# The end of a two-block transformer kernel weighted between panels and turned behind the last one, the even RMS norm multiplied in one operation, and four layer-norm shifts as one rounded product

## The reference, cut to what matters

```python
def layer_norm(x, g, b):
    mu = jnp.mean(x, -1, keepdims=True)
    var = jnp.mean(jnp.square(x - mu), -1, keepdims=True)
    return (x - mu) * lax.rsqrt(var + LN_EPS) * g + b
...
def rmsnorm(x, g):
    y = xf * lax.rsqrt(jnp.mean(xf * xf, axis=-1, keepdims=True) + EPS)
    return (y * g.astype(jnp.float32)).astype(x.dtype)
...
    for l in range(DEPTH):
        hl = rmsnorm(xl, norm_g[l]) * (1.0 + scale[:, None]) + shift[:, None]
        ...
        xl = xl + gate[:, None] * out_l.astype(xl.dtype)
    return rmsnorm(xl, final_g)
```

## Time and profile before

| | us |
|---|---|
| median of 3 runs | 2527.7 (2525.87 to 2528.76) |
| the profiled execution's own time | 2529.48 |
| its span | 2527.7 |
| PE busy | 2487.7 (98% of the span) |
| DVE, POOL, ACT busy | 1450.2, 1081.8, 955.5 |
| mean granted clock of PE | 0.997 |

### The profile page before, as it was taken

How to read it: one execution, slowest core, us unless ns; L and a number is a source line. 1 busy time by engine, 2 the same in 40 slices (tenths; PEclk the granted TensorE clock), 3 DMA queues, 4 the chain that set the end, 5 groups by cost and what they waited for, 6 DMA issues and landing times.

```text
span 2527.7 us, 34143 instructions
## 1 busy us (share of the span) xinstructions
PE 2487.7 (98%) x12624; PEld 2006.3 (79%) x12624; DVE 1450.2 (57%) x2058; ACT 955.5 (38%) x1500; POOL 1081.8 (43%) x718
## 2 busy tenths in 40 slices
PE   8999999999999999999999999999999999999999
PEld 7888887667788887788888877788888888787887
DVE  6545456575765645554555658674343364896553
ACT  5222224554522223432222568653222244463322
POOL 3978874313776735243343402264020056032401
PEclk9999999999999999999999999999999999999999
DMA  8345445311444446244443221145333326533332
GB/s 213 92 128 153 127 123 132 104 23 55 133 130 145 124 134 159 89 134 148 131 125 111 81 80 42 44 149 167 109 108 92 94 76 194 188 124 113 92 92 66
DMA packets 439258, 292.05 MB, mean 116 GB/s; under 512 B 34371, under 2 KB 420218, under 8 KB 435802
## 3 DMA queue, kind: packets, MB, share of 16 engines
q1 hardware_dynamic: 422042, 212.38, 29.9%
q0 software_dynamic: 17088, 77.93, 9.9%
HBM read 272.50 MB, written 20.92 MB: 116 GB/s over the span
## 4 chain that ended last, share of the span: by engine, by line
PE 87%; POOL 5%; DVE 3%; ACT 2%; DMA 1%; issue 1%; SPq 0%; ACTq 0%; POOLq 0%; DVEq 0%
PE ps L784 40%; PE ps L789 20%; PE ps L867 5%; PE ps L895 4%; PE ps L1096 2%; PE ps L1084 2%; POOL SW L3177 1%; POOL NS L3175 1%; PE ps L1532 1%; POOL NS L3174 1%; DMA raw<-in_ffn_w_down 1%; PE ps L1111 1%; PE ps L1385 1%; PE ps L1103 1%; POOL BK L3177 1%
## 5 line engine op out<-in xcount | busy, mean ns | idle before, releaser
L2330 DVE TENSOR_TENSOR wl<-raw,wh 128x1024 fp32r<-128x1024 f32 x376 | 623.6, 1659 | 830.2 <-ACT wh L1758 829.7
L1758 ACT ACTIVATE wh<-raw 128x1024 fp32r<-128x1024 f32 x385 | 408.2, 1060 | 1305.4 <-PE ps L789 1149.7
L784 PE MATMUL ps<-XH,wh 128*128 128x512 f32 x1832 | 718.5, 392 | 0.5 <-ACT wh L1758 0.5
L784 PE MATMUL ps<-XL,wh 128*128 128x512 f32 x1832 | 713.1, 389 | 0.0
L789 PE MATMUL ps<-XH,wl 128*128 128x512 f32 x1832 | 453.2, 389 | 0.0
L784 PEld LDWEIGHTS ps<-XH,wh 128*128 128x128 f32 x1832 | 343.9, 188 | 77.0 <-issue 4.9
L784 PEld LDWEIGHTS ps<-XL,wh 128*128 128x128 f32 x1832 | 343.9, 188 | 72.9 <-issue 2.2
L789 PEld LDWEIGHTS ps<-XH,wl 128*128 128x128 f32 x1832 | 343.8, 188 | 71.7 <-issue 0.4
L3296 POOL TENSOR_TENSOR NS<-AW,CS 128x2048 f32<-128x2048 f32 x32 | 117.7, 3679 | 272.7 <-PE ps L789 233.3
L784 PE MATMUL ps<-HH,wh 128*128 128x512 f32 x528 | 207.3, 393 | 2.2 <-ACT wh L1758 2.2
L784 PE MATMUL ps<-HL,wh 128*128 128x512 f32 x528 | 205.5, 389 | 0.0
(11 more groups left out here) (544 smaller groups left out, 3925.0 us busy)
## 6 DMA issues: line engine op xcount, KB each, us to landing
raw<-in_ffn_w_gu SPq DMA_DIRECT2D x176, 512.0 KB, 3.9
raw<-in_ffn_w_down SPq DMA_DIRECT2D x64, 512.0 KB, 3.9
AW<-in_ada_w POOLq DMA_DIRECT2D x24, 1024.0 KB, 6.5
raw<-in_ffn_w_down SPq DMA_DIRECT2D x32, 384.0 KB, 3.4
BS<-s_b POOLq DMA_DIRECT2D x12, 1024.0 KB, 5.3
raw<-in_odd_w_in SPq DMA_DIRECT2D x24, 512.0 KB, 3.8
raw<-in_even_w_in SPq DMA_DIRECT2D x22, 512.0 KB, 4.5
s_w<-SW POOLq DMA_DIRECT2D x12, 512.0 KB, 6.5
```

The lines of the kernel that those rows point to most:

```text
L784: pe.matmul(ps[:, p % 4, 0:n], wh[:, p % 2, k * P:(k + 1) * P], x[:, k, 0:n], start=k == 0 and x is hi, stop=False)
L1758: act.activation(wh[:, p % 2, :], raw[:, p % 4, :], ACT.Copy).then_inc(w_hi, 1)
L2330: dve.tensor_tensor(wl[:, p % 2, :], raw[:, p % 4, :], wh[:, p % 2, :].bitcast(F32), ALU.subtract).then_inc(w_lo, 1)
```

## The change

Three edits. None adds or removes a panel.

1. **Four shifts.** For ffn0 to ffn3 (not wo0 and wo1) ACT rounds block 0 of `XT` into `XH[:, 0, :]`, which no product reads by then, and PE multiplies it with a rounded column of 1/128 (`PART`, written once by ACT ahead of the first shift): a single-pass fp32r product for a float32 one. PE waits for a new semaphore, `first_hi`. So that the number of semaphores stays, `cmask_in` is merged into `mla_in_s`.
2. **Even RMS norm.** DVE makes `NT = XT * AG * factor` in one operation (no affine behind it). ACT makes `XH = round(NT + MOD)` and, for the even blocks, `NT = NT + MOD` in place for POOL. For the odd blocks DVE makes `XL = (NT + MOD) - XH` in one operation. POOL takes four blocks and DVE four, where it was six and two.
3. **The end.** Behind each panel's square ACT multiplies the block by `final_g` into `XG` (the tile `YO`); DVE does the last block. Behind the last panel PE transposes blocks 0 to 2 at once, then reduces the square of block 7, then transposes blocks 3 to 7; the reductions give one column per 128 tokens (tokens on partitions), so that square root and reciprocal are 128x4 and the spread is gone. The factor is applied behind the transposes, as tokens then lie on partitions: DVE for token blocks 0 and 2, ACT for 1 and 3, in three pieces each (3, 2 and 3 channel blocks). Four DMAs, one for each 128 tokens, 512 KB with rows of 4 KB. The `warm` products there are gone.

```diff
 # PE, shift(stage, j)
-                pe.matmul(ps[:, 4, :], EPS[:, 3:4].broadcast_to([P, P]), XT[:, 0, :], start=True, stop=True).then_inc(ln_mean, 1)
+                if stage in SHIFT_HI:
+                    pe.wait_ge(first_hi, SHIFT_HI.index(stage) + 1)
+                    pe.matmul(ps[:, 4, :], PART[:].broadcast_to([P, P]), XH[:, 0, :], start=True, stop=True).then_inc(ln_mean, 1)
+                else:
+                    pe.matmul(ps[:, 4, :], EPS[:, 3:4].broadcast_to([P, P]), XT[:, 0, :], start=True, stop=True).then_inc(ln_mean, 1)
 # ACT, behind(stage, p, j)
                 if j < KD - 1:
                     cast(BASE[stage] + p + 2)
+                if j == 0 and stage in SHIFT_HI:
+                    if stage == "ffn0":
+                        act.activation(PART[:], EPS[:, 3:4], ACT.Copy)
+                    act.wait_ge(*taken_at(stage, p))
+                    act.activation(XH[:, 0, :], XT[:, 0, :], ACT.Copy).then_inc(first_hi, 1)
 # ACT, rms: the even norm
-                    act.activation(XH[:, d, :], src[:, d, :], ACT.Identity, scale=AG[:, layer, d, 0:1],
-                                   bias=MOD[:, layer, d, 0:1]).then_inc(ln_hi, 1)
+                    if layer == 0:
+                        act.activation(XH[:, d, :], src[:, d, :], ACT.Identity, bias=MOD[:, layer, d, 0:1]).then_inc(ln_hi, 1)
+                        if d not in EVEN_BY_DVE:
+                            act.activation(src[:, d, :], src[:, d, :], ACT.Identity, bias=MOD[:, layer, d, 0:1]).then_inc(ln_aff, 2)
...
 # DVE, rms: the even norm, EVEN_BY_DVE = (1, 3, 5, 7)
+                for d in range(KD + 2 if layer == 0 else 0):
+                    if d < KD:
+                        dve.scalar_tensor_tensor(dst[:, d, :], XT[:, d, :], AG[:, 0, d, 0:1], ps[:, 4, :], ALU.mult, ALU.mult).then_inc(ln_n, 1)
+                    if d - 2 in EVEN_BY_DVE:
+                        dve.wait_ge(ln_hi, 8 * hi + d - 1)
+                        dve.scalar_tensor_tensor(XL[:, d - 2, :], dst[:, d - 2, :], MOD[:, 0, d - 2, 0:1], XH[:, d - 2, :].bitcast(F32), ALU.add, ALU.subtract).then_inc(x_dve, 1)
 # PE, the end: square_columns() is column_means(ACQ) in the place of rms_sum("final")
+            def column_means(src, first, last):
+                for t in range(TT):
+                    mm = pe.matmul(ps[:, 5, t:t + 1], src[:, t * P:(t + 1) * P], ONES[:, 0:1], start=first and t == 0, stop=last and t == TT - 1)
+                return mm
...
+            for d in range(3):
+                turned(d)
+            pe.wait_ge(sq_ready, LN_SQ["final"] + KD)
+            column_means(SQ[:, (LN_SQ["final"] + KD - 1) % 2, :], False, True).then_inc(sq_used, 1)
+            for d in range(3, KD):
+                turned(d)
 # ACT, the end (weighted(at) runs behind each square)
+                if d < KD - 1:
+                    act.activation(XG[:, d, :], XT[:, d, :], ACT.Identity, scale=COL[:, 96 + 64 + d:96 + 65 + d]).then_inc(ln_aff, 1)
+                else:
+                    turned_out(0)
+                    turned_out(2)
...
+            for t in (1, 3):
+                act.activation(XO[:, t, 0:3 * P], XO[:, t, 0:3 * P], ACT.Identity, scale=RSTD[:, t:t + 1])
+            for t in (1, 3):
+                act.wait_ge(out_ps, 5)
+                act.activation(XO[:, t, 3 * P:5 * P].rearrange("p (i c) -> p i c", c=P), turned_rows(3, 2, t), ACT.Identity, scale=RSTD[:, t:t + 1])
+            for t in (1, 3):
+                act.wait_ge(out_ps, KD)
+                act.activation(XO[:, t, 5 * P:].rearrange("p (i c) -> p i c", c=P), turned_rows(5, 3, t), ACT.Identity, scale=RSTD[:, t:t + 1]).then_inc(out_sb, 1)
 # DVE, the end: block 7's weight, the copy of block 1, a 128x4 reciprocal, then the same three pieces for t in (0, 2)
+            dve.tensor_scalar(XG[:, KD - 1, :], XT[:, KD - 1, :], COL[:, 96 + 64 + KD - 1:96 + 64 + KD], None, ALU.mult).then_inc(ln_n, 1)
+            dve.wait_ge(out_ps, 2)
+            dve.tensor_copy(XO[:, :, P:2 * P], ps[:, OUT_BANK[1], :].rearrange("p (t c) -> p t c", t=TT)).then_inc(ln_n, 1)
+            reciprocal(width=TT)
...
 # SP
-            for half in range(2):
-                sp.wait_ge(out_sb, 4 * half + 4)
-                sp.dma_start(rows_out[:, :, half * T:(half + 1) * T], XO[:, :, half * T:(half + 1) * T]).then_inc(out_done, 16)
-            sp.wait_ge(out_done, 32)
+            for t in range(TT):
+                sp.wait_ge(*((ln_n, LAST_N + 3 + t // 2) if t % 2 == 0 else (out_sb, 3 + t // 2)))
+                sp.dma_start(rows_out[:, t, :], XO[:, t, :]).then_inc(out_done, 16)
+            sp.wait_ge(out_done, 16 * TT)
```

More of the change, by code:

```diff
@@ L487, in program @@
         g_out = sem("g_out")
-        cmask_in = sem("cmask_in")
+        first_hi = sem("first_hi")
         qs_hi = sem("qs_hi")
@@ L546, in program @@
         ROOT_NO = {"ffn0": 1, "wo0": 4, "ffn1": 5, "ffn2": 6, "wo1": 7, "ffn3": 8, "even": 9, "odd": 10, "final": 11}
+        SHIFT_HI = ("ffn0", "ffn1", "ffn2", "ffn3")
         SHIFT_AT = {"ffn0": 1, "wo0": 2, "ffn1": 1, "ffn2": 1, "wo1": 3, "ffn3": 1}
@@ L564, in program @@
         XS = {"ffn0": 0, "mla": 8, "wo0": 14, "ffn1": 22, "kv": 28, "ffn2": 28, "nsa": 34, "wo1": 40, "ffn3": 48, "even": 54,
-              "glu": 60, "odd": 66}
-        XD = {"mla": 0, "ffn1": 2, "kv": 4, "ffn2": 4, "nsa": 6, "ffn3": 8, "even": 10, "odd": 12}
+              "glu": 58, "odd": 64}
+        XD = {"mla": 0, "ffn1": 2, "kv": 4, "ffn2": 4, "nsa": 6, "ffn3": 8, "even": 10, "odd": 14}
         BY_DVE = (3, 7)
+        EVEN_BY_DVE = (1, 3, 5, 7)
         LN_COL = {"ffn0": 0, "wo0": 8, "ffn1": 16, "ffn2": 24, "wo1": 32, "ffn3": 40}
@@ L599, in program, with out_at, turned_rows @@
         T_BANK = (1, 6)
+        XG = YO
+        LAST_N = 8 * LN_NO["final"]
+        OUT_BANK = (4, 6, 7)
+        def out_at(d, t):
+            if d < 3:
+                return OUT_BANK[d], t * P
+            first, i = ((0, 1), d - 3) if d < 5 else ((2, 6), d - 5)
+            return first[t % 2] + i // 2, i % 2 * 2 * P + t // 2 * P
+        def turned_rows(d, count, t):
+            bank, col = out_at(d, t)
+            return ps[:].rearrange("p b c -> p (b c)")[:, bank * T + col - t // 2 * P:][:, 0:count * 2 * P].rearrange("p (i h c) -> p i h c", h=2, c=P)[:, :, t // 2]
         block = ctx.enter_context(nc.Block())
@@ L929, in all_of @@
                 def all_of(k):
-                    if stage in XD and k in BY_DVE:
-                        return x_dve, XD[stage] + BY_DVE.index(k) + 1
-                    return x_split, XS[stage] + k + 1 - (sum(e < k for e in BY_DVE) if stage in XD else 0)
+                    by_dve = () if stage not in XD else EVEN_BY_DVE if stage == "even" else BY_DVE
+                    if k in by_dve:
+                        return x_dve, XD[stage] + by_dve.index(k) + 1
+                    return x_split, XS[stage] + k + 1 - sum(e < k for e in by_dve)
                 if stage == "ffn0":
@@ L1861, in rms @@
                 act.wait_ge(sq_used, PE_SQ[stage] + (1 if stage in ADDED else KD))
-                act.activation(ROOT, ps[:, 5, 0:P], ACT.Sqrt, bias=EPS[:, 2:3]).then_inc(sd_ready, 1)
+                width = P if layer is not None or wout is None else TT
+                act.activation(ROOT[:, 0:width], ps[:, 5, 0:width], ACT.Sqrt, bias=EPS[:, 2:3]).then_inc(sd_ready, 1)
                 beside("root")
@@ L2316, in _, with turned_out, weighted @@
                 take("odd", 16 + j, ZO[:, j % 2, :], ACT.Silu)
-            rms("final", lambda d: taken_at("owo", d), wout="owo")
-            for d in range(KD):
+            def turned_out(d):
                 act.wait_ge(out_ps, d + 1)
-                act.activation(XO[:, :, d * P:(d + 1) * P], ps[:, (6, 7, 0, 1)[d % 4], :].rearrange("p (t c) -> p t c", t=TT), ACT.Copy).then_inc(out_sb, 1)
+                act.activation(XO[:, :, d * P:(d + 1) * P], ps[:, OUT_BANK[d], :].rearrange("p (t c) -> p t c", t=TT), ACT.Copy).then_inc(out_sb, 1)
+            def weighted(at):
+                if at[0] != "square":
+                    return
+                d = at[1]
+                if d < KD - 1:
+                    act.activation(XG[:, d, :], XT[:, d, :], ACT.Identity, scale=COL[:, 96 + 64 + d:96 + 65 + d]).then_inc(ln_aff, 1)
+                else:
+                    turned_out(0)
+                    turned_out(2)
+            rms("final", lambda d: taken_at("owo", d), wout="owo", beside=weighted)
+            act.wait_ge(rstd_ready, ROOT_NO["final"])
+            act.wait_ge(out_sb, 2)
+            act.wait_ge(ln_n, LAST_N + 2)
+            for t in (1, 3):
[6 more added lines that the diff above has]
+                act.activation(XO[:, t, 5 * P:].rearrange("p (i c) -> p i c", c=P), turned_rows(5, 3, t), ACT.Identity, scale=RSTD[:, t:t + 1]).then_inc(out_sb, 1)
         @block.vector
@@ L3322, in _ @@
             norm("ffn2")
-            pool.wait_ge(cmask_in, 16)
+            pool.wait_ge(mla_in_s, 96)
             def rest_of_q(j, q):
```

57 lines of the change are left out of this document (35 added, 22 removed).

## The result

The changed kernel takes 2533.52 us (median of 9 runs, 2532.42 to 2537.28) against 2526.07 us for the kernel before on the same chip (9 runs, 2525.63 to 2528.76). The ratio is 1.003, 95% interval [1.0021, 1.0039]: slower, by 7.5 us in the medians. The forecast was 2521.7 and faster. The profiled executions took 2536.54 and, before, 2529.48: both some 3 us over their medians, and 7.1 apart.

A forecast was written before the change was run, and what follows sets the result against it. PE, busy 98% of the span, was taken as the bound. 1.4 + 2.8 + 2.7 = 6.9 us saved gave 2522.6 from the profiled execution or 2520.8 from the median; the middle, 2521.7, was forecast, 8-in-10 range 2517.8 to 2525.5.

The forecast's parts named there:

- the price of the new tile: Shift in ffn0: ACT writing PART takes 0.20 us, cutting that shift's net saving to 0.32; nothing counted for PART's place.
- Part 1: Four shifts: rounded product saves PE time less a new wait; 0.32 + 0 + 0.52 + 0.52 = 1.4 us.
- rivals: Clock stays up (0.2), even norm stays late (0.2), change doesn't do what it says (0.1), transfers don't overlap (0.05).
- PE's 2.25 in ffn1 not grown: ffn1: an earlier PE waits longer than 2.25 us for a late weight panel; no growth would show the forecast wrong.
- Even norm: Pair of panels behind the even norm: 15.47 us becomes 12.7, no waits, 3.4 us of low clock; gain 2.8.
- the old 4.5 of loss: Old even pair: 11.0 us of matmuls plus 1.1 of waits plus 3.4 lost to the low clock makes 15.5.
- a slack of 0.1 to 0.9: New even pair: DVE has each XL block ready 0.1 to 0.9 us before PE wants it, so no wait.
- The rival that the clock stays up: Even pair: PE has no idle time left, the clock doesn't fall; gain 8.6 us, time 2520.0; chance 0.2.
- End: Behind the last panel: first transfer issued at 2517.5 instead of 2520.31, span end at 2524.9; gain taken as 2.7 us.
- The rival of transfers that don't overlap: End: four 512 KB transfers of 3.9 us each run one after another; slower, 2530.3 us; chance 0.05.

The follow-up runs named there:

- e1: The changed kernel with all three edits, but PART a column of ST, so that no tile moves: 2519.27 us, ratio 0.997 against the kernel before.
- e2: The kernel before with only a dead tile of 32 bytes per partition where the change puts PART, no edits: 2542.16 us, ratio 1.0065.
- e5: The kernel before with the shifts edit alone, PART a column of ST, no tile moved: 2525.39 us, ratio 0.9993.
- e12: All three edits, no tile moved but YH and YL, 384 bytes on: 2517.56 us, ratio 0.9959 against the kernel before.
- e4: The changed kernel with a dead 32 bytes more ahead of the first-phase, feed-forward and context-overlay tiles: 2524.85 us, ratio 0.9993 against the kernel before.
- e6: The kernel before with the even norm edit alone, no tile moved: 2523.26 us, ratio 0.9983.
- e9: All three edits, no tile moved but YH and YL, 128 bytes on: 2516.43 us, ratio 0.9961 against the kernel before.
- e11: All three edits, AG put ahead of wh, so weights, XH and XL start 128 bytes later; HH and YH stay: 2528.27 us, ratio 1.0001 against before.

## Why the prediction was wrong

**The step that failed** is the price of the new tile. Part 1 costed it as "In ffn0 ACT writes `PART` in between, 0.20", and the sum ends with "1.4 + 2.8 + 2.7 = 6.9 us". A term is missing, put at nothing without a reason: where `PART` lies. It costs 14.2 (after less e1; 15.5 when each is taken against its own runs of before) or 14.9 (e2 less before). With it: 2521.7 + 14.2 = 2535.9, 2.4 above what was measured; without it, e1 ran 2519.3, in the predicted range. None of the rivals held it, since each asked what the edited instructions do, and this one slows 2112 that no line of the diff names. The profile of before had the clue: streams of the same form at 389 (`XL`, `HL`) and 395 (`YL`) in the groups of its matmuls, though nothing they waited for differed. I hadn't asked why.

**Shifts**, 1.4 predicted, 1.1 measured in the traces. ffn1 gave nothing, as said, and ffn0 0.35 for 0.32. ffn2 gave 0.1 less and ffn3 0.15 less than 0.52; PE takes 0.31 for the rounded product's slot, not 0.23. My sign of error, "PE's 2.25 in ffn1 not grown", tells nothing: the wait grew to 4.12, but the panel's transfer was issued 6.35 later, no later than all else there, and then took 24.40 for 22.62. In e1 the wait is 2.3, and it varies from 1.9 to 2.9 in the kernels whose feed-forward tiles stayed.

**Even norm**, 2.8 predicted, 2.9 in after (15.47 to 12.54): the number was luck, as two errors cancelled. I split the old 4.5 of loss into 1.1 of waits and 3.4 of clock and let the new pair keep 1.7 for the clock. But the table shows that the old pair takes 14.88 to 14.91 with the clock low for 3.4 us or not at all: `XL` set its pace, and what the clock lost wasn't added to the waits but stood in their place (0.77 + 0.68 + 0.98 + 0.23 = 2.7 of idle in e5 for 1.1 in before). With 6.8 us of low clock it grows by 0.5 to 0.6, not by the 3.4 of my sum. In the new pair PE sets the pace more nearly: 3.4 us at the low clock cost 0.6 to 0.9, where I had 1.7. In e12, where the whole stretch lies in the pair, eight matmuls take 0.427 for 0.227, 1.6 in all, and the pair is 0.9 longer. The pairs at full clock lose part of the difference to `XL`: in e1, e4, e6, e9 and e11 PE stands idle once for 0.28 to 0.33, named XL, which I had excluded with a slack of 0.1 to 0.9. The rival that the clock stays up came true in the traces of five of the nine kernels with the new norm. The same small products stand ahead of the pair in all of them, so they don't make the clock fall by themselves, as my step had it. Nor is the fall tied to idle time here: in e5 PE was idle four times and kept 1.00; in after the clock fell at 2105.3, and from 2085 until then PE had been idle once, for 0.23 us. The rule of the Trainium skill that I quoted ("TensorE: Matmul & The Clock Gate", "What's actually happening"), that the low clock comes after an idle stretch, does not fit this fall either. What sets it is open.

**End**, 2.7 predicted, 3.3 measured. Counted from the last but one matmul of the last panel (2510.37 before, 2520.79 after), the first issue came 7.0 later where I had 2517.5 - 2510.37 = 7.1 and before had 9.9; the steps up to it were right within 0.1 in sum (the reciprocal ended 0.3 earlier than I had it, and the pieces behind it took 0.2 longer). The transfers gave the other 0.4, at about 400 GB/s instead of 380: 6.9 from the first issue to the span's end for 7.4. The rival of transfers that don't overlap is refuted. The rule of the Trainium skill for transfers of 1 MiB or more ("DMA: Bandwidth & Descriptors", section "Rules for kernel authors") didn't decide here: four of 512 KB went faster than two of 1 MB. But their rows also grew from 2 KB to 4 KB, and no run separates the two.

**What causes the conflict** is shown only so far: the time of a matmul depends on the distance of two addresses mod 256, with another best distance for 256 columns than for 512, and e11 excludes the streamed address alone and the weights' alone. That the stream and the load of the next weights meet in the same part of the memory would fit, but no run tests it. The Trainium skill has nothing of this: "SBUF — State Buffer", section "SBUF: two separate sides", has TensorE never wait on anyone, and section "A bandwidth-pool intuition that's wrong (but worth ruling out)" gives the weight load a second, independent read port. The traces have 227 against 229 to 236 ns for the same instruction, with PE never idle; here the measurement decides.

## What to carry to other kernels

A new tile, however small, is an edit of every tile behind it: put it last, or into a spare column, and compare the mean time of unedited matmuls before and after. Put streamed operands of 512 columns a multiple of 256 bytes from the weights they meet; here that was worth 1 to 4% of each matmul, and two tiles that had never been placed so gave 2 us more. For 256 columns 64 bytes was the best of five distances tried, so measure each width by itself. And where an engine waits for another, don't add what its slow clock costs to the waits: ask which of the two ends last.

## What the runs showed of the hardware that was not expected

- A matmul of 512 rounded columns takes 227 ns start to start when streamed tile and weights start at the same place mod 256, and 229 to 236 ns at every other multiple of 32. One of 256 columns takes 120 ns there and 115.5 at 64 bytes.
- The low clock came in stretches of 3.4 or 6.8 us ahead of the tail, and at other places from one kernel's trace to the next: at 441.6, 1015.0 and 2093.6 in before, at 36.9, 651.2, 999.4 and 2105.3 in after, at 991.1 alone in e1.
- Four transfers of 512 KB in rows of 4 KB moved 397 to 406 GB/s in the full windows; the two of 1 MB in rows of 2 KB 362 to 399.
- Eight matmuls of 512 columns at the 1.2 GHz level took 427 ns each from start to start (e12), 1.6 us more than at the full clock, and the pair was only 0.9 longer.
